# A mixture-of-experts layer whose weights arrive in transfers of 2 MB into 8 slots, instead of 1 MB into 17 slots

## The chip, the cores and the metric

The kernel runs on one core of a Trainium2 chip. The metric is the device time of one execution in microseconds (us). The time before is the median of three runs.

## The reference

One transformer layer on 512 tokens of width 1024, in float32: attention and a state-space branch side by side, an output projection, and then a feed-forward part in which every token is sent to 4 of 32 experts. Nearly all of the bytes and three quarters of the time are in that last part:

```python
def moe_ffn(h, w_router, b_router, w_gate, b_gate, w_up, b_up, w_down, b_down):
    logits = (t @ w_router + b_router).astype(jnp.float32)
    top_val, top_idx = lax.top_k(logits, TOP_K)            # TOP_K = 4 of 32
    top_w = jax.nn.softmax(top_val, axis=-1)
    ...
    def expert_block(args):
        xb, e = args                                       # rows of one expert
        g = xb @ w_gate[e] + b_gate[e]                     # 1024 x 1024
        u = xb @ w_up[e] + b_up[e]                         # 1024 x 1024
        g = jnp.minimum(g, SWIGLU_LIMIT)
        u = jnp.clip(u, -SWIGLU_LIMIT, SWIGLU_LIMIT)
        act = g * jax.nn.sigmoid(SWIGLU_ALPHA * g) * (u + 1.0)
        return act @ w_down[e] + b_down[e]                 # 1024 x 1024
```

Every expert has three matrices of 1024 x 1024 float32, 4 MB each. All 32 experts are read, so 384 MB pass from HBM to the core's memory once.

## The kernel before

The kernel is written engine by engine with explicit semaphores. Its first part (some 350 us) computes attention and the state-space branch. Then the router sorts the experts by how many tokens they got, and the expert part runs over 32 positions `j`, one expert at each. An expert's tokens are counted in groups of 32; a position has a fixed number of groups, in this order (a constant of the program, `GROUPS_AT`):

```python
[3, 3, 2, 3, 2, 3, 3, 2, 3, 3, 2, 3, 2, 3, 2, 2, 4, 2, 2, 4, 2, 2, 4, 2, 2, 2, 5, 2, 1, 5, 1, 1]
```

**TensorE.** The products of position `j` come in stages: gate of `j`, up of `j`, down of `j-1`. A stage runs through the 1024 rows of its matrix in 8 blocks of 128 (`k`), and for each block and each group it issues matmuls on the block's 1024 columns. The tokens are the stationary operand, the weights stream. A stage with 5 groups is done as two visits, 4 groups and then 1, both over the same weights. Small pieces of other work (transposes of the next tokens, one-hot products that sort them) are hooked in at fixed blocks `k`, and they stay at the same blocks.

**The weights.** A matrix is cut into pieces of `KP` blocks of 128 rows; before, `KP = 2`, so a piece is 256 rows, 1 MB, and `PIECES = 4` make a matrix. `STREAM` lists all pieces in the order of use: 384 of them before. Piece `n` goes into slot `n % NRING`, with `NRING = 17`; `RING_AT` says which part of the memory `ring` (and, for one slot, `rest`) a slot is. The text counts pieces of 1 MB from 0, before and after.

**The queue of loads.** SyncE (SP) issues all the loads of weights, in the order of `STREAM`, from one instruction stream. Before it issues a load it waits until the slot's last piece is used up (`piece_used`): for the last piece of a stage that is the end of the stage, for the others a semaphore that TensorE raises after the last visit's last matmul on that piece. A load raises a semaphore of its slot when it has landed whole, and TensorE waits for that at the piece's first block (`pe.wait_ge(s_raw[slot], ...)`, in `product`). The first loads are issued during the first part of the kernel, as the memory under their slots comes free, by the `load(n, ...)` calls that stand one by one in the code.

**The other engines.** After gate and up, VectorE and ScalarE compute the activation. After down, VectorE adds the bias, ScalarE scales the rows (L990), and GpSimd (POOL) adds them into the output with an indirect DMA for each group (L752, "scatter" below), and fetches the next tokens' rows with another (L740, "gather"). The next position's result may only be written over `yrow` when the scatters before have landed.

Of the kernel before, what the change touches and what calls it, by code (L numbers as in the profile page):

```python
# [14 lines left out]
P = 128  # L15
SEQ, DM = 512, 1024
NT = SEQ // P
KT = DM // P
# [16 lines left out]
DE = DM  # L35
# [1 line left out]
LIMIT, ALPHA = 7.0, 1.702  # L37
GRID_W = 64
IW = 52
KP = 2  # L40
PIECES = KT // KP
NRING = 17
SLOT = 4096
NQ = 4
QW = DM // NQ
# [93 lines left out]
UNITS = product_units()  # L139
STREAM = weight_stream()  # L140
SETS = 3
RING_AT = (0, 1, 16, 4, 5, 14, 15, 6, 7, 8, 9, 12, 13, 2, 3, 10, 11)
OVER_USES = [("d", 0), ("r", 0), ("x", 0), ("x", 1), ("a", 0), ("a", 1)]


# [96 lines left out]
def hybrid_layer(nc, d, out, hn):  # L242
    ctx = ExitStack()
    with ctx:
# [4 lines left out]
        big = ctx.enter_context(nc.sbuf_tensor("ring", [P, 8 * SLOT], F32))  # L249
# [55 lines left out]
        xs_w = take(NT * SW)  # L305
# [41 lines left out]
        bias_x, hT_x = xpad_w[:, 0:3 * QW], xpad_w[:, 3 * QW:4 * QW]  # L347
        btab, onehot_x = bias_w[:, 0:3 * QW], bias_w[:, 3 * QW:3 * QW + NT * TOK]
        onehot = const[:, 0:NT * P]
        slots = [big[:, n * KP * DE:(n + 1) * KP * DE] for n in range(16)] + [xs_w]  # L350
        pieces = [cut(slots[n], KP, DE) for n in RING_AT]

        rt = qT_w.rearrange("p (a b) -> p a b", b=P)
# [109 lines left out]

        WEIGHTS = ("w_gate", "w_up", "w_down")

        def piece_source(m, e, r):

            return d[WEIGHTS[m]][0, e].rearrange("(r p k) n -> r p k n", p=P, k=KP)[r]

        BIASES = ("b_gate", "b_up", "b_down")  # L470

# [118 lines left out]
        def _(sp):  # L590
            def load(n, e):

                m, j, r = STREAM[n]
                turn, slot = at_piece[m, j, r]
                if turn:
                    piece_used(sp, n - NRING)
                sp.dma_start(pieces[slot], piece_source(m, e, r)).then_inc(s_raw[slot], 16)  # L597

            sp.dma_start(const, d["const"]).then_inc(s_const, 16)
            for t in range(NT):  # L600
# [23 lines left out]
            sp.dma_start(w_out, w_out_d).then_inc(s_wout, 16)  # L624
            sp.dma_start(wr, d["w_router"][0].rearrange("(k p) n -> p k n", p=P)).then_inc(s_wr, 16)
            load(0, 0)
            load(1, 0)

            wait_full(sp, f"sb{NT - 1}")
            sp.dma_start(gffn, bc(d["norm_ffn"][0])).then_inc(s_gffn, 16)  # L630
            for t in range(NT):
                if t == NT - 1:

                    sp.wait_ge(s_ys, NT)
                    wait_full(sp, f"yf{NT - 1}")
                    for n in (2, 3, 4):
                        load(n, 0)
                    wait_full(sp, f"p{NPAIR - 1}b")
                    load(5, 0)
                    sp.wait_ge(s_of, NPAIR)  # L640
                    load(6, 0)
                wait_taken(sp, f"op{t}a")
                wait_taken(sp, f"op{t}b")
                sp.dma_start(out_d[t * P:(t + 1) * P, :], x1[:, t, :]).then_inc(s_ost, 16)
                if t == NT - 1:
                    for n in range(7, 13):
                        load(n, STREAM[n][1])
                sp.wait_ge(s_h, t + 1)
                sp.dma_start(hn_d[t * P:(t + 1) * P, :], hrw).then_inc(s_hst, 16)

            sp.wait_ge(s_ost, 16 * NT)
            for n in (13, 14):
                load(n, STREAM[n][1])
            sp.wait_ge(s_hst, 16 * NT)
            wait_full(sp, f"lg{NT - 1}")
            for n in (15, 16):
                load(n, STREAM[n][1])

            held = {}
            for n in range(NRING, len(STREAM)):  # L660
                m, j, r = STREAM[n]
# [8 lines left out]
            def over_loads(q):  # L670

                sp.wait_ge(s_done, q + 1)
                e = over_expert(sp, q)
                for m in range(3):
                    src = d[BIASES[m]][0, e]
                    for k in range(NQ):
                        sp.dma_start(bias_x[k * TOK:(k + 1) * TOK, m * QW:(m + 1) * QW],
                                     bc(src[k * QW:(k + 1) * QW], TOK)).then_inc(s_bover, 16)
                for m in range(3):
                    for r in range(PIECES):  # L680
                        turn, slot = over_piece(q, m * PIECES + r)
                        sp.dma_start(pieces[slot], piece_source(m, e, r)).then_inc(s_raw[slot], 16)

            overflow(sp, over_loads)

# [807 lines left out]
        def _(pe):  # L1493
# [246 lines left out]
                                dmask[vi.b][0:c, 0:vi.G, :].rearrange("p a b -> p (a b)"), start=True, stop=True), use)  # L1740

            def kp_rows(ap, blocks):
                return ap.rearrange("p (r i k) -> p r i k", r=blocks, k=KP)

            def turn_rows(vi):

                pe.wait_ge(s_gath[vi.b], 16 * (vi.gathers + 1))
                c = vi.G * TOK
                for h in range(2):
                    use = vi.turns["x", h]  # L1750
                    ps = turning(use)
                    for k in range(4):
                        r, kk = divmod(4 * h + k, KP)
                        last = T.transpose(ps[:, k * c:(k + 1) * c], kp_rows(hrow[vi.b][0:c, :], PIECES)[:, r, :, kk],  # L1754
                                           ident[0:c, 0:c])
                    turned(last, use)

            def turn_act(vi):

                pe.wait_ge(s_act_, vi.n + 1)  # L1760
                for h in range(last_part(vi) + 1):
                    use = vi.turns["a", h]
                    ps = turning(use)
                    rows = kp_rows(ub_b[vi.b][:, 0:vi.G * QW], vi.G)
                    for n in range(min(2, vi.G - 2 * h) * KP):
                        g, kk = divmod(n, KP)
                        last = T.transpose(ps[:, n * P:(n + 1) * P], rows[:, 2 * h + g, :, kk], ident)
                    turned(last, use)

# [116 lines left out]
```

## Time and profile before

| | us |
|---|---|
| median of 3 runs | 1445.22 (1445.13 to 1448.4) |
| the profiled execution, its own time | 1445.26 |
| its span, first to last instruction | 1443.4 |
| TensorE matmul busy | 1309.5 (91%) |
| TensorE loading its stationary operand (PEld, overlapped) | 810.8 (56%) |
| VectorE busy | 443.7 (31%) |
| ScalarE busy | 220.2 (15%) |
| GpSimd busy | 193.3 (13%) |
| DMA, mean over the span | 309 GB/s of 446.16 MB |
| TensorE clock, mean granted | 0.969 |

TensorE's busy time is the time in which at least one matmul was in flight, which is not the same as running at its peak. The DMA share of a stretch is that of the 16 DMA engines; it can come out slightly over 1. "SPq" is the instruction queue of SyncE, and a row of it is a load being issued.

### The profile page before, as it was taken

Reading aid. Unit: us, or ns where it says so; the run is one execution under the profiler, and the core shown is the slowest. Engines: PE = TensorE matmul, PEld = TensorE weight load, DVE = VectorE, ACT = ScalarE, POOL = GpSimd, SP = SyncE. Lnnn points to the kernel's source line nnn. Section 1 sums busy time; section 2 is a strip of 40 time slices with the busy share of each in tenths; the row PEclk is TensorE's granted clock in tenths of the full one; section 3 lists DMA queues with packets and bytes.
Section 4 is the critical chain, followed back from the end, with each engine's and each line's share of the span. In section 5 each row is a group of like instructions: output and inputs, shape, how many; then the busy total and the mean of one; then the engine's idle time right before and its main releaser. Section 6 shows DMA issues by size and latency. Waiting matters only on the chain.

```text
span 1443.4 us, 40133 instructions
## 1 busy us (share of the span) xinstructions
PE 1309.5 (91%) x18029; PEld 810.8 (56%) x18029; DVE 443.7 (31%) x1030; ACT 220.2 (15%) x491; POOL 193.3 (13%) x148
## 2 busy tenths in 40 slices
PE   5999989996799999999998988999989989995992
PEld 3466676664556666666555555655656655663651
DVE  3653576553322222222221211221222221311211
ACT  2123244331101111000100110110010101101100
POOL 0000310000101211111221111121121131011021
PEclk9999999998799999999999999999999999997996
DMA  8000320018899999999999999999999999999692
GB/s 347 2 1 0 153 99 1 30 42 337 311 335 380 392 387 382 391 393 399 397 394 401 398 411 396 410 400 399 411 396 405 408 395 408 403 402 384 263 408 92
DMA packets 79342, 446.16 MB, mean 309 GB/s; under 512 B 13218, under 2 KB 21474, under 8 KB 30018
## 3 DMA queue, kind: packets, MB, share of 16 engines
q1 hardware_dynamic: 64050, 426.37, 73.4%
q0 software_dynamic: 15120, 17.20, 5.6%
q8 instruction: 144, 2.36, 0.7%
q14 instruction: 28, 0.23, 0.0%
HBM read 433.29 MB, written 14.94 MB: 311 GB/s over the span
## 4 chain that ended last, share of the span: by engine, by line
PE 45%; SPq 41%; DMA 5%; issue 3%; DVE 3%; POOL 1%; ACT 1%; DVEq 0%; POOLq 0%; ACTq 0%
SPq L597 41%; PE pair L1795 22%; PE pair L1549 8%; PE pair L1533 4%; PE pair L1510 2%; DMA out<-rest 2%; DMA rest<-in_w_gate 2%; PE pair L1641 2%; DVE rest L1033 1%; PE pair L1754 1%; PE pair L1653 1%; POOL ring L700 1%; PE pair L1730 1%; PE pair L1697 1%; POOL out L752 1%
## 5 line engine op out<-in xcount | busy, mean ns | idle before, releaser
L1795 PE MATMUL pair<-ring,rest 128*32 128x256 f32 x14832 | 840.3, 381 | 34.4 <-DMA ring<-in_w_down 16.4
L1795 PEld LDWEIGHTS pair<-ring,rest 128*32 128x32 f32 x14832 | 479.4, 110 | 343.8 <-issue 25.8
L1033 DVE TENSOR_TENSOR rest<-pair,rest 128x512 f32<-128x512 f32 (+5 forms) x122 | 90.7, 743 | 491.6 <-PE pair L1795 428.4
L752 POOL DMA_INDIRECT out<-rest x82 | 128.3, 1564 | 805.5 <-ACT rest L990 739.4
L1549 PE MATMUL pair<-ring 128*128 128x512 f32 (+1 forms) x320 | 125.3, 550 | 0.0
L990 ACT ACTIVATE rest<-rest 128x256 f32<-128x256 f32 x82 | 36.5, 500 | 560.8 <-DVE rest L1033 560.8
L1549 PEld LDWEIGHTS pair<-ring 128*128 128x128 f32 x320 | 60.3, 190 | 60.4 <-issue 58.8
L1033 DVE TENSOR_TENSOR rest<-rest 128x512 f32<-128x512 f32 (+7 forms) x98 | 62.4, 650 | 34.8 <-ACT rest L972 26.7
L1795 PE MATMUL pair<-rest 128*32 128x256 f32 x912 | 55.7, 384 | 16.2 <-DVE rest L1033 13.0
L972 ACT ACTIVATE rest<-rest 128x512 f32<-128x512 f32 (+3 forms) x34 | 24.4, 718 | 292.2 <-DVE rest L1342 292.2
L1754 PE MATMUL pair<-rest 64*128 64x64 f32 (+3 forms) x272 | 41.3, 295 | 16.2 <-ACT rest L982 14.9
L1533 PE MATMUL pair<-ring 128*128 128x512 f32 x128 | 55.4, 594 | 0.0
L1754 PEld LDWEIGHTS pair<-rest 64*128 64x128 f32 (+3 forms) x272 | 35.9, 212 | 30.0 <-issue 28.6
L1510 PE MATMUL pair<-rest,ring 128*128 128x128 f32 (+1 forms) x193 | 29.2, 301 | 24.1 <-DMA ring<-in_ssm_norm 11.3
L1309 DVE TENSOR_SCALAR rest<-pair 64x1 int32<-64x1 f32 (+3 forms) x34 | 5.2, 152 | 146.3 <-issue 137.6
L1795 PEld LDWEIGHTS pair<-rest 128*32 128x32 f32 x912 | 28.7, 110 | 36.5 <-DVE rest L1033 13.4
L740 POOL DMA_INDIRECT rest<-normed_rows,rest x34 | 34.8, 1025 | 98.0 <-DVE rest L1309 67.3
L1322 DVE TENSOR_SCALAR rest<-pair,rest 128x2 int32<-128x2 f32 (+3 forms) x34 | 7.5, 221 | 130.4 <-PE pair L1739 130.4
L1510 PEld LDWEIGHTS pair<-rest,ring 128*128 128x128 f32 (+1 forms) x193 | 23.4, 154 | 38.0 <-issue 21.7
L700 POOL TENSOR_TENSOR ring<-rest 128x512 f32<-128x512 f32 x16 | 21.8, 1389 | 168.6 <-PE pair L1575 136.1
L964 ACT ACTIVATE rest<-pair 128x256 f32<-128x256 f32 (+3 forms) x68 | 28.2, 428 | 88.1 <-PE pair L1754 85.5
L1533 PEld LDWEIGHTS pair<-ring 128*128 128x128 f32 x128 | 24.2, 190 | 30.5 <-issue 30.5
(171 smaller groups left out, 827.6 us busy)
## 6 DMA issues: line engine op xcount, KB each, us to landing
ring<-in_w_up SPq DMA_DIRECT2D x121, 1024.0 KB
ring<-in_w_gate SPq DMA_DIRECT2D x120, 1024.0 KB
ring<-in_w_down SPq DMA_DIRECT2D x120, 1024.0 KB
rest<-in_w_gate SPq DMA_DIRECT2D x8, 1024.0 KB
rest<-in_w_down SPq DMA_DIRECT2D x8, 1024.0 KB
rest<-in_w_up SPq DMA_DIRECT2D x7, 1024.0 KB
ring<-in_w_in SPq DMA_DIRECT2D x1, 4160.0 KB, 15.5
ring<-in_x SPq DMA_DIRECT2D x8, 512.0 KB, 5.8
```

The source lines that it names most:

```text
L597: sp.dma_start(pieces[slot], piece_source(m, e, r)).then_inc(s_raw[slot], 16)
L700: nc.gpsimd.tensor_tensor(out=sm[k % 2], in0=times(mask, HPG), in1=over(da[:, c, di * SH + g * HPG:di * SH + (g + 1) * HPG], P), op=ALU.mu ...
L740: p.indirect_dma_start(out=hrow[vi.b][0:c, :], out_offset=None, in_=hn_d, in_offset=bass.IndirectOffsetOnAxis(ap=idx_g[vi.b][0:c, :].bitca ...
L752: p.indirect_dma_start(out=out_rows, out_offset=bass.IndirectOffsetOnAxis(ap=sidx[vi.ring][:, g:g + 1].bitcast(I32), axis=0), in_=yrow[:, ...
L990: ins = nc.scalar.activation(y, y, ACT.Copy, scale=wv[vi.ring][:, g:g + 1])
L1033: return v.tensor_tensor(out=out, in0=a, in1=b, op=op)
L1510: last = T.transpose(ps[:, n * P:n * P + k], a, ident[0:k, 0:k])
L1533: last = T.matmul(ps[:, :], w_in[:, k, XBC0 + ch * P:XBC0 + (ch + 1) * P], hTm[:, k, :], start=(k == 0), stop=(k == KT - 1))
L1549: last = T.matmul(ps[:, 0:b - a], src[:, k, t * P:(t + 1) * P], w[:, k, a:b], start=(k == 0), stop=(k == KT - 1))
L1641: last = T.matmul(bank[7][:, head * HD:(head + 1) * HD], probsT[p % 2 * 2 + h][:, kt, :], vs[:, kt, kv * HD:(kv + 1) * HD], start=(kt == 0 ...
L1754: last = T.transpose(ps[:, k * c:(k + 1) * c], kp_rows(hrow[vi.b][0:c, :], PIECES)[:, r, :, kk], ident[0:c, 0:c])
L1795: last = T.matmul(ps[q * TOK:(q + 1) * TOK, g * QW:(g + 1) * QW], x, pieces[slot][:, kk, q * QW:(q + 1) * QW], start=(k == 0 and g % 2 == ...
```

## The change

`KP` becomes 4: a piece is now 512 rows, 2 MB, and two of them make a matrix. `NRING` becomes 8, so the ring holds 16 MB, where it held 17. `RING_AT` names the eight 2 MB parts of `ring`; the 1 MB slot in `rest` is no longer used. The source of a piece is described so that each partition still receives, for every block of 256 rows, two rows that lie side by side in HBM: a transfer is 128 partitions x 2 runs of 8 KB, where it was 128 partitions x 1 run of 8 KB. Transposes of the tokens keep their arithmetic of two (`k=2` written out), so the products are the same. The first loads are issued at the same places of the program, regrouped.

```diff
-KP = 2
+KP = 4
 PIECES = KT // KP
-NRING = 17
+NRING = 8
...
-RING_AT = (0, 1, 16, 4, 5, 14, 15, 6, 7, 8, 9, 12, 13, 2, 3, 10, 11)
+RING_AT = (0, 2, 7, 3, 4, 6, 1, 5)
...
-        slots = [big[:, n * KP * DE:(n + 1) * KP * DE] for n in range(16)] + [xs_w]
+        slots = [big[:, n * KP * DE:(n + 1) * KP * DE] for n in range(NRING)]
         pieces = [cut(slots[n], KP, DE) for n in RING_AT]
...
+        def halves(piece):
+            return piece.rearrange("p (a k) n -> p a (k n)", a=2)
+
         def piece_source(m, e, r):
 
-            return d[WEIGHTS[m]][0, e].rearrange("(r p k) n -> r p k n", p=P, k=KP)[r]
+            return d[WEIGHTS[m]][0, e].rearrange("(r a p k) n -> r p a (k n)", a=2, p=P, k=KP // 2)[r]
...
-                sp.dma_start(pieces[slot], piece_source(m, e, r)).then_inc(s_raw[slot], 16)
+                sp.dma_start(halves(pieces[slot]), piece_source(m, e, r)).then_inc(s_raw[slot], 16)
...
             load(0, 0)
-            load(1, 0)
...
-                    for n in (2, 3, 4):
-                        load(n, 0)
+                    load(1, 0)
                     wait_full(sp, f"p{NPAIR - 1}b")
-                    load(5, 0)
                     sp.wait_ge(s_of, NPAIR)
-                    load(6, 0)
+                    load(2, 0)
...
-                    for n in range(7, 13):
+                    for n in range(3, 6):
                         load(n, STREAM[n][1])
...
-            for n in (13, 14):
-                load(n, STREAM[n][1])
+            load(6, STREAM[6][1])
...
-            for n in (15, 16):
-                load(n, STREAM[n][1])
+            load(7, STREAM[7][1])
```

The queue of SyncE around the start of the expert part, where the first slots are used again; `ring` and `rest` are the memories, `in_w_gate`, `in_w_up` and `in_w_down` the three weights, L597 the loads of weights. Before:

```order
L649 DMA normed_rows<-ring 128x1024
L597 DMA ring<-in_w_up 128x2048 x3
L597 DMA ring<-in_w_down 128x2048 x3
L597 DMA rest<-in_w_down 128x2048
L571 TENSOR_LOAD rest
L571 ISA x2
L597 ISA
L597 DMA ring<-in_w_gate 128x2048
```

The same place after the change, where L600 are the loads of weights:

```order
L649 DMA normed_rows<-ring 128x1024
L600 DMA ring<-in_w_up 128x2x2048 x2
L600 DMA ring<-in_w_down 128x2x2048 x2
L574 TENSOR_LOAD rest
L574 ISA x2
L600 ISA
L600 DMA ring<-in_w_gate 128x2x2048
L600 ISA
```

What was two loads is one load of two runs per partition, and the four loads of a matrix are two. No load has passed another kind of instruction. The first load that has to wait for a slot to be used up is piece 17 before (the second of the four loads of `in_w_down`, behind piece 16 which goes into the seventeenth slot), and pieces 16 and 17 together after.

## Rows read from the trace of the kernel before

**Rows 1.** TensorE's waits, 383 to 690 us, all of them: total, times, longest us

```profile
PE pair L1767 <- DVE rest L1360: 1.4, 1, 1.4
```

**Rows 2.** TensorE's waits, 690 to 1212 us: total, times, longest us

```profile
PE pair L1795 <- DMA ring<-in_w_down: 16.4, 19, 2.0
PE pair L1795 <- DMA ring<-in_w_up: 11.3, 9, 2.0
PE pair L1739 <- DMA ring<-in_w_up: 4.7, 5, 1.3
PE pair L1795 <- DMA ring<-in_w_gate: 3.8, 6, 0.6
```

**Rows 3.** TensorE's waits, 1212 to 1443 us

```profile
PE pair L1754 <- ACT rest L982: 14.9, 1, 14.9
PE pair L1795 <- DVE rest L1033: 13.0, 1, 13.0
```

**Rows 4.** Stretches: length, busy PE PEld DVE ACT POOL, PEclk, DMA share, GB/s

```profile
383.00:413.00 30.00, 28.62 (x488) 17.56 (x483) 7.24 (x19) 2.69 (x5) 1.08 (x2) 1.00 0.90 330
413.00:430.00 17.00, 17.00 (x302) 10.34 (x295) 4.32 (x11) 1.61 (x3) 0.84 (x1) 1.00 0.93 342
430.00:566.00 136.00, 136.00 (x2342) 82.71 (x2336) 34.21 (x90) 15.53 (x33) 25.45 (x18) 1.00 1.03 388
690.00:1212.00 522.00, 480.22 (x8061) 290.21 (x8064) 121.55 (x329) 53.37 (x109) 81.70 (x58) 1.00 1.02 402
```

**Rows 5.** SyncE's waits in 380-430, 430-560, 560-690 and 1200-1400 us

```profile
SPq L597 <- PE pair L1795: 54.8, 16, 16.4
...
SPq L597 <- PE pair L1795: 94.9, 50, 3.4
...
SPq L597 <- PE pair L1795: 0.5, 1, 0.5
...
SPq L597 <- PE pair L1795: 89.5, 40, 15.9
```

**Rows 6.** Timeline of SyncE: the issues of pieces 25 to 28, one by one

```profile
408.54 0.33 SPq L597 DMA_DIRECT2D ring<-in_w_up  x1
411.13 0.33 SPq L597 DMA_DIRECT2D ring<-in_w_up  x1
414.63 0.33 SPq L597 DMA_DIRECT2D ring<-in_w_up  x1
417.22 0.34 SPq L597 DMA_DIRECT2D ring<-in_w_down  x1
```

**Rows 7.** Timeline of TensorE, pieces 306 to 309: start, us, [idle before <- releaser]

```profile
1206.78 1.93 PE L1795 MATMUL pair<-ring,rest 128*32 128x256 f32 x32 [0.53 <-DMA ring<-in_w_down]
1209.27 1.93 PE L1795 MATMUL pair<-ring,rest 128*32 128x256 f32 x32 [0.56 <-DMA ring<-in_w_down]
1211.87 1.94 PE L1795 MATMUL pair<-rest 128*32 128x256 f32 x32 [0.67 <-DMA rest<-in_w_gate]
1213.74 0.74 PE L1767 MATMUL pair<-rest 128*128 128x128 f32 x4
1214.41 1.94 PE L1795 MATMUL pair<-rest 128*32 128x256 f32 x32
```

**Rows 8.** The chain that ended last, at piece 308: start, us, what

```profile
1184.00 27.74 DMA rest<-in_w_gate
```

**Rows 9.** DMA queue q1 in 1417.0 to 1417.2 us: packets, MB, share of 16 engines

```profile
q1 hardware_dynamic: 2, 0.00, 0.6%
```

**Rows 10.** Timeline of SyncE from piece 361 on, to piece 383

```profile
1343.92 2.06 SPq L597 DMA_DIRECT2D ring<-in_w_up  x3
1346.51 18.36 SPq L597 DMA_DIRECT2D ring<-in_w_down  x4
1365.62 2.87 SPq L597 DMA_DIRECT2D ring<-in_w_gate  x4
```

**Rows 11.** Timeline of TensorE where pieces 364 and 380 are first used

```profile
1376.67 7.55 PE L1795 MATMUL pair<-ring,rest 128*32 128x256 f32 x136
...
1423.37 3.66 PE L1795 MATMUL pair<-ring,rest 128*32 128x256 f32 x64 [1.06 <-issue]
```

**Rows 12.** The chain that ended last: three waits for scatters

```profile
1298.99 12.94 DMA out<-rest
...
1402.37 13.00 DMA out<-rest
...
1423.77 3.77 DMA out<-rest
```

**Rows 13.** DMA queues in 1299 to 1312 us, during the first of them

```profile
q1 hardware_dynamic: 596, 4.36, 82.8%
q0 software_dynamic: 551, 0.50, 23.9%
```

**Rows 14.** Stretches, as Rows 4: a 4 MB transfer, 1 MB transfers alone, the clock

```profile
171.00:186.00 15.00, 13.87 (x114) 13.28 (x113) 14.31 (x16) 4.78 (x8) 8.14 (x6) 1.00 1.04 407
672.00:689.00 17.00, 17.00 (x305) 10.29 (x307) 4.75 (x10) 2.06 (x5) 0.64 (x1) 1.00 1.01 416
1312.00:1321.00 9.00, 7.41 (x54) 4.68 (x58) 3.33 (x15) 3.16 (x7) 2.62 (x2) 0.51 0.95 365
```

More of the change, by code:

```diff
@@ L681, in over_loads @@
                         turn, slot = over_piece(q, m * PIECES + r)
-                        sp.dma_start(pieces[slot], piece_source(m, e, r)).then_inc(s_raw[slot], 16)
+                        sp.dma_start(halves(pieces[slot]), piece_source(m, e, r)).then_inc(s_raw[slot], 16)
             overflow(sp, over_loads)
@@ L1742, in kp_rows @@
             def kp_rows(ap, blocks):
-                return ap.rearrange("p (r i k) -> p r i k", r=blocks, k=KP)
+                return ap.rearrange("p (r i k) -> p r i k", r=blocks, k=2)
             def turn_rows(vi):
@@ L1752, in turn_rows @@
                     for k in range(4):
-                        r, kk = divmod(4 * h + k, KP)
-                        last = T.transpose(ps[:, k * c:(k + 1) * c], kp_rows(hrow[vi.b][0:c, :], PIECES)[:, r, :, kk],
+                        r, kk = divmod(4 * h + k, 2)
+                        last = T.transpose(ps[:, k * c:(k + 1) * c], kp_rows(hrow[vi.b][0:c, :], KT // 2)[:, r, :, kk],
                                            ident[0:c, 0:c])
@@ L1764, in turn_act @@
                     rows = kp_rows(ub_b[vi.b][:, 0:vi.G * QW], vi.G)
-                    for n in range(min(2, vi.G - 2 * h) * KP):
-                        g, kk = divmod(n, KP)
+                    for n in range(min(2, vi.G - 2 * h) * 2):
+                        g, kk = divmod(n, 2)
                         last = T.transpose(ps[:, n * P:(n + 1) * P], rows[:, 2 * h + g, :, kk], ident)
```

## The prediction

> **What bounds the kernel now.** I first looked for who waits for weights. TensorE's waits, cut into three stretches, give the picture. From 383 to 690 us it never waits for a transfer; its one idle stretch of note is 1.4 us [rows 1]. From 690 to 1212 us all its long waits are for landing weights; the four rows shown are 36 us and the smaller ones bring it to about 42 [rows 2]. After 1212 us it waits 14.9 and 13.0 us for ScalarE and VectorE, and not for weights [rows 3].
>
> Then I asked what the transfers do meanwhile. In 690 to 1212 us the DMA engines are busy all the time and move 402 GB/s; from 430 to 566 us they are as busy (388 GB/s), although TensorE is busy too; only before that are they short of work, at 330 and 342 GB/s and a share of 0.90 and 0.93 [rows 4]. SyncE's waits say why: until 430 us, and mostly until 560, each load waits for TensorE to use up the slot; from 560 to 690 there is one such wait of 0.5 us, and for 690 to 1200 the query had no row at all. They come back after 1200 us (89.5 us) [rows 5].
>
> So the expert part is one chain with three links. Until about 430 us TensorE frees slots and the stream of weights follows it. From there to 1212 us the stream runs by itself at its full rate, first with data in reserve, then with TensorE waiting for it. At 1211.87 us TensorE starts position 26, which has 5 groups [rows 7], and from there to the end TensorE and its scatters set the time. The load it started on had been issued at 1184.00 us and took 27.74 us to land [rows 8]: some ten pieces were queued ahead, so what SyncE does late by a few us there costs nothing. A delay of the stream before 430 us, or of the landing at 1212 us, is passed on to the end in full; elsewhere it is not.
>
> **The change part by part.**
>
> *Fewer slots and coarser release, at the start of the stream.* Before, piece n is issued when n-17 is used up. After, pieces n and n+1 (n even) go out together when both n-16 and n-15 are used up, which is the moment at which piece n+2 was issued before. So the first block of each load goes out two issues later, and the second block one issue later. Pieces 25 to 28 were issued at 408.54, 411.13, 414.63 and 417.22 us [rows 6]: an issue is 2.6 to 3.5 us. One piece transfers in 2.5 us (1209.27 to 1211.87 is 2.6, and 1211.87 to 1214.41 is 2.54) [rows 7]. Where the stream was starved, the second block of a pair ends later by one issue plus the block ahead of it, 2.6 + 2.5 = 5.1 us. Where there already was a block in reserve, it ends later by one issue alone, 2.6 us. By the shares of rows 4 the stream passes from the one to the other about 413 to 430 us. I take the middle, **+3.8 us**, and keep 0 (the reserve was already deeper) to 5.1 for the range. The seventeenth slot that is lost is in this sum: it is piece 16, no longer on board when TensorE starts.
>
> *After 430 us.* The later issues of the same rule cost nothing while loads are queued: at 1184 us the issue stands 27.74 us ahead of the landing [rows 8], and a pair goes out at most two pieces, some 6 us, later. If that cover were gone, each us late would be a us of the total, up to 1212.
>
> *Waiting for the whole 2 MB at 1212 us.* Position 26 can now start only when 308 and 309 have landed. TensorE touched 309 at 1214.41, 2.54 us after 308 [rows 7]; it had not waited for it, so the landing lay at or before that. Before the landing of 308, pieces came each 2.5 us, so 309 is expected at 1214.4: **+2.5 us** (bounds 0 and 2.6). What follows needs a pair each 7 us of work (four groups: two pieces of 3.5), and a pair lands in 5, so it happens once.
>
> *Half the completion writes.* Each load ends on each DMA engine with a small write to its semaphore. Two such packets alone in 0.2 us are 0.6% of 16 engines' time [rows 9]: 0.006 x 16 x 200 / 2 = 9.6 ns. From piece 26 to 308 there are 141 fewer on each engine: **-1.4 us**.
>
> *Work on TensorE, VectorE and the rest.* The matmuls, the hooks and their blocks are the same; 192 waits and as many signals fewer are not on a path with a row: in 383 to 690 us, where data was always there, no idle stood before a piece [rows 1]. 0.
>
> *The end.* After 1212 us slots are late by the same rule, most of all behind stages of 5 groups, whose four pieces are released together. The worst is the pair 364, 365: before, 364 was issued at 1346.51 us and the next three only around 1363; all four ended by 1364.9 [rows 10]. After, the pair waits for the issue time of 366, about 1363.7. Two blocks are 5 us, plus a start of about 1, plus the completion: landed by 1371. TensorE comes to piece 364 inside the row that starts at 1376.67 us [rows 11], about 2 us into it, so 7 to 8 us are left. From there the stream carries one block more than before (364 was already on board), so the last pair lands some 3 us later than the last piece did; it was on board by about 1417.5 (two completion packets at 1417.0 to 1417.2 are its last [rows 9]), and the last stage runs its four pieces in 3.66 us from 1423.37 [rows 11]: the last pair is wanted at 1425.2, 4.7 us after 1420.5. So the end is covered, by 5 us at the tightest, and moves as a block. 0; if the cover fails, 1 us for 1 us.
>
> *Sum.* 3.8 + 2.5 - 1.4 = +4.9 us. The profiled execution took 1445.26 us, of which 1443.4 is its span; the median of the runs is 1445.22, so nothing is to be corrected. **1450.2 us.**
>
> **A rule weighed against the rows.** A 4 MB transfer (of the output weights, in runs 512 KB apart) moved 407 GB/s, and 1 MB pieces by themselves 416 GB/s [rows 14]; so neither a larger transfer nor one that jumps between blocks is seen to run at another rate, and the sum has 0 for it. The Trainium skill (DMA: Bandwidth & Descriptors, section Bandwidth) gives 341 GB/s for single transfers of 1 MB and 425 GB/s for 16 MB, from a fixed 2 us each. By that rule doubling the size would cut the stream's time noticeably; the rows disagree, since 1 MB pieces queued behind each other lose nothing of that kind.
>
> **The rivals.**
>
> *A: the stream gets faster.* Per-load losses that I can't see are halved. For: the mean of 402 GB/s in 690 to 1212 us is under the 416 of the clean stretch [rows 4, 14]. Against: the scatters and gathers explain that, and rows 14 show no gain by size. Were it 2% (402 to 410), the 800 us from 413 to 1212 would shrink by 16 us, well inside the 42 us that TensorE waits: 1450.2 - 16 = 1434. It is faster than before by over 0.3% as soon as the rate gains 1.2%. Chance 0.10.
>
> *B: scatters land later.* The waits for scatters are on the chain, 12.94 and 13.00 us for four each while weights flow, against 3.77 for one alone [rows 12]. In the first, the scatters' queue q0 has 23.9 parts to 82.8 of the weights' q1 [rows 13]. So of 3.2 us per scatter 0.8 is its own and 2.4 is turns given to the weights. If a turn doubles with the transfer, a scatter takes 5.6 us, four take 22.5, and both waits grow by 9.5: 1450.2 + 19 = 1469. Against: the runs of 8 KB stay as they are; a turn may well be one run. Chance 0.12. The Trainium skill (DMA: Bandwidth & Descriptors, section Queues, rings and completion order) has the engines change queues only after a whole packet of typically 9 to 17 descriptors, and by that rule a load of twice the descriptors would take longer turns; no row here shows whose packets they are.
>
> *C: the clock falls.* Two short pauses per 2 MB become one: 2.0 us at most before [rows 2], so up to 3 or 4 us after. The clock stayed at 1.00 (2.4 GHz) throughout 690 to 1212 us [rows 4], but stood at 0.51, near its 1.2 GHz level, for the 7.2 us of work after the 13 us wait [rows 14]. Were it low when position 26 begins, that costs half of 7.2, 3.6 us: 1454. Elsewhere the stream hides it. Chance 0.10.
>
> *D: the reserve hides the start.* If the stream was saturated before 413 us, the 3.8 falls away: 1445.3 + 2.5 - 1.4 = 1446.4, no change that can be told. For: TensorE's own pace there is close to the stream's. Against: the share of 0.93 up to 430 us. Chance 0.25.
>
> **How the numbers follow.** The forecast case, 1449.0 to 1451.5 by its bounds (one issue, or one issue and a block, with the 2.5 and the -1.4), has 0.43. About 0.3% (4.3 us) is what a measurement can tell from no change, so the line is at 1449.6. The forecast case gives 0.33 to slower and 0.10 to same; D 0.25 to same; B and C 0.22 to slower; A 0.10 to faster. Together 0.10, 0.35, 0.55. The range of 1440 to 1464 takes in the forecast case, C, D and the milder parts of A and B.
>
> **What would show it.** (1) TensorE's waits for weights: none before about 670 us, then pauses about twice as long and half as many, some 45 us in all. (2) Position 26 begins at 1216 to 1217 us. (3) The rest, from there to the end, is as long as before, 1443.4 - 1211.9 = 231.5 us of span; a longer one means B, seen in waits of over 20 us for `out<-rest`, or a failed cover at the end, seen as waits for weights after 1217. (4) GB/s in the middle stretch 402 within 1%; 406 or more is A. (5) A granted clock under 1.00 between 690 and 1212 us is C. The prediction is wrong if the rate of the stream moves with the transfer's form, each 1% being 8 us.

## The result: slower by 0.6 to 0.7%, and where it went

The changed kernel took 1454.35 us (median of 8 runs) beside 1445.18 us for the kernel before: ratio 1.0069, 95% interval [1.0051, 1.0087]. Measured again on another occasion: 1452.33 us beside 1445.31, ratio 1.0059 [1.0043, 1.0074]. The ratios are those on record with their intervals; the quotients of the medians are 1.0063 and 1.0049. Its first profiled execution took 1454.72 us, with a span of 1452.8 us; the second 1451.29 us, span 1449.5.

The stretches of the changed kernel, with the columns of [rows 4], come first:

```profile
383.00:413.00 30.00, 28.62 (x488) 17.50 (x480) 7.24 (x19) 2.68 (x5) 0.97 (x1) 1.00 0.78 290
413.00:430.00 17.00, 17.00 (x301) 10.35 (x294) 3.59 (x10) 1.61 (x3) 0.96 (x1) 1.00 1.00 362
690.00:1212.00 522.00, 488.54 (x8109) 294.28 (x8105) 122.37 (x329) 55.38 (x114) 83.24 (x59) 0.98 1.02 402
```

Until 413 us the stream of weights moves 290 GB/s, where it moved 330; the DMA share has gone from 0.90 to 0.78. In the middle the rate is 402 GB/s, as before. So the bytes are late from the start and not slower on the way. The timeline of SyncE shows the new steps of the start. Each load is now 2 MB, so the row with `x2` is two loads and 4 MB, and the time from 404.42 to 411.96 and on to 424.46 is what TensorE needs to use up whole pairs. Before, pieces went out singly, 2.6 to 3.5 us apart [rows 6].

```profile
404.42 0.38 SPq L600 DMA_DIRECT2D ring<-in_w_gate  x1
411.96 6.46 SPq L600 DMA_DIRECT2D ring<-in_w_up  x2
424.46 0.38 SPq L600 DMA_DIRECT2D ring<-in_w_down  x1
```

SyncE's waits in 380-430, 560-690, 690-1200 and 1200-1400 us, which answer to [rows 5]:

```profile
SPq L600 <- PE pair L1793: 54.0, 7, 19.4
...
SPq L600 <- PE pair L1793: 27.9, 9, 6.0
...
SPq L600 <- PE pair L1793: 97.1, 38, 6.9
...
SPq L600 <- PE pair L1793: 145.0, 29, 20.9
```

After 560 us SyncE now waits for slots again and again (97.1 us in 38 waits between 690 and 1200 us), where before it hardly did. It looks bad and costs nothing there: DMA share and GB/s are those of before, because a load still has 33 us from issue to landing. A wait of an engine that runs far ahead is no loss.

TensorE's waits, first 383 to 690 us [rows 1], then 690 to 1212 us [rows 2], then 1220 to 1453 us [rows 3]:

```profile
PE pair L1793 <- DMA ring<-in_w_gate: 3.0, 1, 3.0
PE pair L1793 <- DMA ring<-in_w_down: 2.8, 3, 1.9
PE pair L1765 <- DVE rest L1358: 1.4, 1, 1.4
...
PE pair L1793 <- DMA ring<-in_w_down: 17.8, 9, 3.2
PE pair L1793 <- DMA ring<-in_w_up: 10.2, 6, 2.6
PE pair L1793 <- DMA ring<-in_w_gate: 3.9, 4, 1.4
...
PE pair L1752 <- ACT rest L980: 15.8, 1, 15.8
PE pair L1793 <- ACT rest L980: 13.8, 1, 13.8
PE pair L1793 <- issue: 1.1, 1, 1.1
```

There are fewer and longer waits for weights (9 for `w_down`, where there were 19), and none near the end. TensorE's timeline at the start of the expert part and around position 26 [rows 7]:

```profile
379.13 6.06 PE L1793 MATMUL pair<-ring,rest 128*32 128x256 f32 x76 [0.63 <-issue]
...
1208.96 3.66 PE L1793 MATMUL pair<-ring,rest 128*32 128x256 f32 x64 [0.46 <-DMA ring<-in_w_down]
1213.76 3.66 PE L1793 MATMUL pair<-ring,rest 128*32 128x256 f32 x64 [1.14 <-DMA ring<-in_w_down]
1218.82 1.93 PE L1793 MATMUL pair<-ring,rest 128*32 128x256 f32 x32 [1.40 <-DMA ring<-in_w_gate]
```

and the same first row in the kernel before:

```profile
378.08 6.27 PE L1795 MATMUL pair<-ring,rest 128*32 128x256 f32 x76 [0.63 <-issue]
```

Position 26 begins at 1218.82 us, 6.95 us later than before (1211.87). 1.05 us of that existed already when the expert part began (379.13 against 378.08). That start varies by itself: in thirteen profiles of kernels that share everything ahead of it except the first loads it lay between 375.5 and 379.1 us. So I compare **the time from the first matmul of the expert part to the start of position 26**: 833.8 us before, 839.7 after, so 5.9 us; 839.1 in the second profile, so 5.3.

The rest, from position 26 to the end of the span, took 234.0 us (before 231.5). The chain that ended last has here, with [rows 8] and [rows 12]:

```profile
1185.63 33.06 DMA ring<-in_w_gate
...
1305.93 13.80 DMA out<-rest
...
1409.99 13.87 DMA out<-rest
...
1425.23 6.35 PE pair L1793 x64
...
1433.44 3.75 DMA out<-rest
```

The two long waits for scatters are 0.9 us longer each. So 9.4 us of difference between the two profiled spans are 1.05 ahead of the expert part, 5.9 up to position 26, 1.7 in scatter waits, and 0.7 in the work between them. The 64 matmuls behind the second wait alone took 6.35 us instead of 5.17; in the second profile they took 5.17 again.

### The profile page after: what moved, and what is told of

It reads as the page before. It is cut to its first block, busy times and chain, and to the rows that moved or that the text cites. A ratio compares the mean times of both kernels' runs of the same rounds, so it can differ in the third digit from the quotient of the medians.

```text
span 1452.8 us, 39702 instructions
## 1 busy us (share of the span) xinstructions
PE 1316.4 (91%) x18029; PEld 813.2 (56%) x18029; DVE 443.8 (31%) x1030; ACT 220.0 (15%) x491; POOL 193.1 (13%) x148
## 4 chain that ended last, share of the span: by engine, by line
PE 64%; DMA 21%; SPq 8%; DVE 3%; issue 2%; POOL 1%; ACT 1%; DVEq 0%; POOLq 0%; ACTq 0%
PE pair L1793 39%; DMA ring<-in_w_gate 10%; PE pair L1547 8%; SPq L600 7%; DMA ring<-in_w_up 5%; PE pair L1531 4%; DMA ring<-in_w_down 3%; DMA out<-rest 2%; PE pair L1508 2%; PE pair L1752 2%; PE pair L1639 2%; PE pair L1765 1%; PE pair L1728 1%; DMA ring<-in_w_in 1%; DVE rest L1031 1%
## 5 line engine op out<-in xcount | busy, mean ns | idle before, releaser
L1793 PE MATMUL pair<-ring,rest 128*32 128x256 f32 x15744 | 897.2, 385 | 56.2 <-DMA ring<-in_w_down 21.8
L1793 PEld LDWEIGHTS pair<-ring,rest 128*32 128x32 f32 x15744 | 510.1, 111 | 389.9 <-issue 45.2
L1531 PEld LDWEIGHTS pair<-ring 128*128 128x128 f32 x128 | 24.2, 190 | 30.5 <-issue 30.5
L1367 DVE STREAM_SHUFFLE rest<-rest 128x256 f32<-128x256 f32 (+1 forms) x64 | 37.9, 592 | 0.0
L1297 DVE TENSOR_SCALAR rest<-rest 128x64 f32<-128x64 f32 (+3 forms) x136 | 26.3, 259 | 25.0 <-DVE rest L1031 19.0
```

The costliest lines, as they stand in the source:

```text
L1367: lk(v.stream_shuffle(out=bias_x[:, a * QW:b * QW], in_=btab[:, a * QW:b * QW], mask=[j] * TOK))
L1531: last = T.matmul(ps[:, :], w_in[:, k, XBC0 + ch * P:XBC0 + (ch + 1) * P], hTm[:, k, :], start=(k == 0), stop=(k == KT - 1))
L1793: last = T.matmul(ps[q * TOK:(q + 1) * TOK, g * QW:(g + 1) * QW], x, pieces[slot][:, kk, q * QW:(q + 1) * QW], start=(k == 0 and g % 2 == ...
```

## The experiments

All kernels were timed beside the kernel before on the same chip. Its median there was 1445.18 us for ring16, pair_issue, pair_wait and ring7, 1445.31 for after_again, split26, one_two_one and half_loads, 1446.80 for rows_by_two and rows_by_four, and 1447.48 for the last two; each ratio is to its own. The columns behind the ratio are read from the one profiled execution: from the first expert matmul to position 26, the sum of the two long scatter waits in the chain (before: 12.94 + 13.00), and from position 26 to the end of the span.

| kernel | us | ratio, 95% interval | to position 26 | against before | scatters | from position 26 to the end |
|---|---|---|---|---|---|---|
| before | 1445.18 | | 833.8 | | 25.9 | 231.5 |
| changed | 1454.35 | 1.0069 [1.0051, 1.0087] | 839.7 | +5.9 | 27.7 | 234.0 |
| after_again | 1452.33 | 1.0059 [1.0043, 1.0074] | 839.1 | +5.3 | 26.9 | 232.8 |
| ring16 | 1447.83 | 1.0016 [0.9996, 1.0036] | 836.5 | +2.7 | 25.9 | 232.6 |
| pair_issue | 1452.72 | 1.0043 [1.0022, 1.0065] | 838.4 | +4.6 | 26.0 | 231.1 |
| pair_wait | 1447.85 | 1.0011 [0.9993, 1.0028] | 836.3 | +2.5 | 27.2 | 234.3 |
| ring7 | 1462.23 | 1.0121 [1.0074, 1.0168] | 844.8 | +11.0 | 27.4 | 237.2 |
| split26 | 1451.42 | 1.0056 [1.0034, 1.0077] | 837.9 | +4.1 | 27.1 | 232.5 |
| one_two_one | 1444.63 | 0.9992 [0.9977, 1.0007] | 832.7 | -1.1 | 26.0 | 232.4 |
| half_loads | 1951.50 | 1.3456 [1.3398, 1.3513] | | | | |
| rows_by_two | 1443.70 | 0.9972 [0.9945, 0.9999] | 833.8 | 0.0 | 24.6 | 230.9 |
| rows_by_two_again | 1442.71 | 0.9975 [0.9957, 0.9993] | 833.4 | -0.4 | 24.2 | 230.3 |
| rows_by_four | 1457.91 | 1.0063 [1.0040, 1.0086] | 849.4 | +15.6 | 20.5 | 231.0 |
| two_in_four | 1450.94 | 1.0037 [1.0017, 1.0057] | 839.9 | +6.1 | 24.0 | 231.3 |

Two profiles of one kernel differ by 0.4 to 0.6 us to position 26, by up to 0.7 in the scatter waits and by up to 1.2 in the last column. The medians are worse: single executions of the kernel before lay between 1442 and 1454 us.

### One slot less (ring16)

```diff
-NRING = 17
+NRING = 16
...
-RING_AT = (0, 1, 16, 4, 5, 14, ...
+RING_AT = (0, 1, 4, 5, 14, ...
...
```

> One part alone: 16 slots of 1 MB, everything else as before. Theory 1 (the loss is made where the stream of weights is starved, until about 430 us, and the start of position 26 passes it on): each piece goes out one issue of TensorE later, 2.6 us, so position 26 begins at 1214.5 instead of 1211.9 and the time is 1447.8 us. Clock 1.00 in 690 to 1212 us and scatter waits of 12.9 and 13.0 us as before. Theory 2 (what was lost is the seventeenth slot, the form of the loads matters little): most of the 7 us of the changed kernel, 1451 us or more. Theory 3 (the form of the loads costs it all: 2 MB transfers and their completion): no change, 1445.2 us.

Position 26 came 2.7 us later (2.6 expected), the median rose by 2.6 us; the interval of its ratio still takes in 1, so it is the profile that shows it, where the spread is 0.6. The seventeenth slot is worth one issue of TensorE, since it decides how far the stream is ahead when it stops being starved.

### Issue in pairs (pair_issue)

```diff
-                if turn:
+                if turn and n % 2 == 0:
                     piece_used(sp, n - NRING)
+                    piece_used(sp, n + 1 - NRING)
...
```

The 16 slots of ring16 are in this kernel too.

> 16 slots of 1 MB, and the two loads of a pair are both issued only when both slots are used up; transfers stay 1 MB with a semaphore each, and TensorE waits for each by itself. Theory 1: the lag of the whole start, 5.1 us and up to 1 us more; nothing for the whole pair at position 26, and the lag does not shrink in the middle, since there are as many completion writes as before: position 26 begins at 1217 to 1218 us and the time is 1450.4 to 1451.4 us, 2.6 to 3.6 us over the kernel with 16 slots. No pause of TensorE over 2.3 us in 690 to 1212 us, clock 1.00. Theory 3 (form of the loads): as the kernel with 16 slots, within 1 us.

4.6 us in the profile, where 5.1 to 6.1 was expected, and a median of 1452.72 us for 1450.4 to 1451.4. Its timeline at position 26, against [rows 7], has the old rhythm of single waits near 0.6 us; only the time has moved:

```profile
1212.39 1.93 PE L1796 MATMUL pair<-ring,rest 128*32 128x256 f32 x32 [0.56 <-DMA ring<-in_w_down]
1214.97 1.93 PE L1796 MATMUL pair<-ring,rest 128*32 128x256 f32 x32 [0.65 <-DMA ring<-in_w_gate]
```

So the lost slot and the rule of issue together, in transfers of 1 MB, make four fifths of the delay up to position 26; over ring16 the rule adds 1.9 us, somewhat less than one issue. Its median (1452.72) is higher than its profiled execution (1447.94) for reasons the profile can't show; I go by the profile's 4.6.

### Wait for pairs (pair_wait)

```diff
-                    if first:
-                        pe.wait_ge(s_raw[slot], 16 * (pturn + 1))
+                    if first and r % 2 == 0:
+                        for pturn, sl in (piece(m, r), piece(m, r + 1)):
+                            pe.wait_ge(s_raw[sl], 16 * (pturn + 1))
```

> The kernel before, with 17 slots and loads of 1 MB, but TensorE waits for both pieces of a pair before it begins the first. Theory 1: position 26 begins 2.5 us later, at 1214.4 us, and the time is 1447.7 us. In the middle the pauses are as in the changed kernel, up to 3.0 to 3.3 us, and the clock falls there some times to its half (mean 0.98), which costs nothing that shows at position 26. Theory 4 (the fallen clock costs time, the stream does not hide it): 1449 us or more, position 26 at 1216 or later.

2.5 us to position 26, as expected. The median of 1447.85 us, near the expected 1447.7, is no second proof: in the profile 2.8 us more come behind position 26, and the expert part happened to begin 2.5 us earlier than in the kernel before (375.54 against 378.08). The rows at position 26 show two things:

```profile
1205.31 3.66 PE L1796 MATMUL pair<-ring,rest 128*32 128x256 f32 x64 [1.18 <-DMA ring<-in_w_down]
1211.82 2.57 PE L1796 MATMUL pair<-rest 128*32 128x256 f32 x32 [2.85 <-DMA ring<-in_w_gate]
1214.33 1.13 PE L1767 MATMUL pair<-rest 128*128 128x128 f32 x4
```

The wait is 2.85 us, where before it was 0.67. And the 32 matmuls behind it take 2.57 us instead of 1.94, the four transposes 1.13 instead of 0.74: the granted clock was at half from 1212.8 to 1216.3 us, just behind the pause, exactly where it is not hidden (rival C's place). These two rows cost 1.0 us of the 234.3 us from position 26 to the end, and the next 32 matmuls (2.40 us instead of 1.94) another half. In the middle, where the stream has slack, the clock fell twice and nothing is seen of it at position 26.

### One pair fewer (ring7)

```diff
-NRING = 8
+NRING = 7
...
-RING_AT = (0, 2, 7, 3, 4, 6, 1, 5)
+RING_AT = (0, 2, 7, 3, 4, 6, 1)
...
```

> The changed kernel with 7 slots of 2 MB instead of 8. Theory 1: a pair goes out two issues of TensorE later still, 5.2 us where the stream is starved, which now lasts longer than to 430 us; position 26 begins at about 1224 us and the time is about 1459.6 us. The cover of the last stages (5 to 6 us) gets short there; a wait for weights after 1224 us would add to it. Theory 5 (the start had a reserve that swallowed most of it, and the 7 us have another source): under 1457 us.

844.8 us to position 26, 5.1 to 5.8 us more than the changed kernel in its two profiles (5.2 expected): two issues again. The time is 2.6 us over the expected 1459.6, and TensorE's waits after 1222 us name what is new, a wait for weights and a longer gap at the end:

```profile
PE pair L1792 <- issue: 3.3, 1, 3.3
PE pair L1792 <- DMA ring<-in_w_up: 1.8, 1, 1.8
```

So the cover of the last stages, put at 5 us at its tightest with 8 slots, is used up with 7, as far as the one wait of 1.8 us for weights shows; what makes the gap of 3.3 us (1.1 before), no row says.

### Position 26 begins on the first half (split26)

```diff
+                if n == SPLIT:
+                    for h, s in enumerate((s_raw[slot], s_half)):
+                        sp.dma_start(halves(pieces[slot])[:, h:h + 1],
+                                     piece_source(m, e, r)[:, h:h + 1]).then_inc(s, 16)
+                    return
...
+                        if first and kk == KP // 2 and vi.j == 26 and m == 0 and r == 0:
+                            pe.wait_ge(s_half, 16)
```

> The changed kernel, but the first load of position 26 (the pair 308, 309) goes as two transfers of 1 MB with a semaphore each, and TensorE begins on the first. Theory 1: position 26 begins 2.5 us earlier than in the changed kernel, and the time is 1451.9 us. Counted from the first matmul of the expert part, which lay between 375.5 and 379.1 us in the profiles so far, it begins 837.2 us later (839.7 in the changed kernel, 833.8 before). If the wait for the whole pair costs nothing because TensorE catches up later, the time stays at 1454.4 us.

Only 1.2 to 1.8 us came back, not 2.5. The timeline says why:

```profile
1206.00 3.66 PE L1801 MATMUL pair<-ring,rest 128*32 128x256 f32 x64 [0.56 <-DMA ring<-in_w_down]
1210.66 5.39 PE L1801 MATMUL pair<-ring,rest 128*32 128x256 f32 x96 [1.00 <-DMA ring<-in_w_down]
```

The x96 are the 64 matmuls of the pair before and the first 32 of position 26, with no wait between: the first half had landed. (Position 26 has no row of its own here; its start, 1214.1 us, is 32 matmuls before the end of this one.) TensorE was held by its wait for the whole pair before it. With pairs throughout, the last wait costs 1.5 us, and 1 us of the 2.5 belongs to the one ahead.

### 1 MB where it counts, 2 MB between (one_two_one)

```diff
+RING_16 = tuple(s for s in RING_AT if s < 16)
+SWITCH = 4 * NRING
+DOUBLE = range(80, 300, 2)
+def slot_of(n):
+    return RING_AT[n % NRING] if n < SWITCH else RING_16[(n - SWITCH) % 16]
...
```

> 1 MB pieces in 17 slots while the stream is starved, as before; from piece 68 the same pieces in 16 slots, from 80 to 299 in transfers of 2 MB that are issued and waited for whole, and 1 MB again from piece 300, so also at position 26. Theory 1: neither the start nor position 26 loses anything and 110 completion writes go: 1.06 us less, position 26 begins 832.7 us after the first matmul of the expert part and the time is 1444.1 us. The clock dips of the changed kernel appear in the middle without a price. If transfers of 2 MB cost something by themselves in the full stream, it is over 1446 us.

No loss: ratio 0.9992, so a transfer of 2 MB costs nothing in the full stream; the whole price is at the start and at the place where TensorE catches up for the last time. Its 832.7 us is what was expected with 110 fewer completion writes. That is 1.1 us under 833.8, not much over the 0.6 between two profiles of one kernel; the next runs test the price of a write directly and find none, so what made the 1.1 us stays open.

### The price of a completion write (half_loads, rows_by_two, rows_by_four)

half_loads, and under it rows_by_two (rows_by_four has 4 for 2, and 64 for 32):

```diff
-                sp.dma_start(pieces[slot], piece_source(m, e, r)).then_inc(s_raw[slot], 16)
+                for a in (0, 64):
+                    sp.dma_start(pieces[slot][a:a + 64],
+                                 piece_source(m, e, r)[a:a + 64]).then_inc(s_raw[slot], 16)
...
+                for a in range(2):
+                    sp.dma_start(pieces[slot][a::2], piece_source(m, e, r)[a::2]).then_inc(s_raw[slot], 16)
...
-                        pe.wait_ge(s_raw[slot], 16 * (pturn + 1))
+                        pe.wait_ge(s_raw[slot], 32 * (pturn + 1))
```

> The kernel before, with each piece of 1 MB loaded as two transfers of 64 rows, so there are twice as many completion writes; packets, slots and waits stay. If a completion write costs the stream 9.6 ns (which is behind the 1.4 us that the changed kernel was to gain), the stream loses 9.6 ns for each of some 280 pieces between 430 us and the start of position 26: that start lies 2.7 us later from the first matmul of the expert part (836.5 instead of 833.8), and the time is 1447.9 us. If the write costs nothing in a full stream: 833.8 and 1445.2 us. If the size of a load sets the stream's rate by a fixed cost of each (rival A): 1450 us or more.

It answered another question. All its stretches are starved though the DMA share is full:

```profile
690.00:1212.00 522.00, 367.97 (x5524) 199.53 (x5528) 81.53 (x212) 37.05 (x75) 54.89 (x39) 0.94 1.02 273
```

273 GB/s instead of 402, by writing to rows 0 to 63 in one transfer and 64 to 127 in the next. The Trainium skill (SBUF — State Buffer, section Door 1: The DMA port swizzle) has a DMA's bandwidth depend on how many of 16 ports its partitions reach, and by its formula 64 neighbouring rows reach 8. The trace agrees in direction. That the rate is more than half of 402 may come from neighbouring transfers, to the two halves, being under way together; no run shows that.

> The kernel before, with each piece of 1 MB loaded as two transfers, one of the even and one of the odd rows, so each transfer writes across the whole memory and not into one half of its rows. Twice as many completion writes, packets of 8 KB as before. If the half rows made the transfers slow (8 KB packets of 0.50 us instead of 0.32 with 64 neighbouring rows), that is gone. If a completion write costs 9.6 ns of the full stream: position 26 begins 836.5 us after the first matmul of the expert part and the time is 1447.9 us. If it costs nothing: 833.8 and 1445.2 us. If each transfer has a fixed cost of its own in the stream, 1450 us or more.

Every second row restores the rate (401 GB/s in 690 to 1212 us). And with twice as many completion writes position 26 begins 833.8 us after the first matmul, to the tenth as before; 833.4 in the second profile below. The two rows:

```profile
377.65 6.54 PE L1798 MATMUL pair<-ring,rest 128*32 128x256 f32 x72 [0.63 <-issue]
...
1211.45 1.94 PE L1798 MATMUL pair<-rest 128*32 128x256 f32 x32 [0.64 <-DMA rest<-in_w_gate]
```

836.5 was expected at 9.6 ns each. **So a completion write costs the full stream nothing that can be seen.** The row on which I had priced it [rows 9] gives its duration on an engine that has nothing else to do, and that isn't its price in a full queue. That packets overlap there would explain it; no run shows how.

> The same with four transfers for each piece, of every fourth row, so four times as many completion writes as before. At 9.6 ns each: 8.2 us more of stream from 430 us to position 26, which begins 842.0 us after the first matmul of the expert part; the time is 1453.4 us. If they cost nothing: 833.8 and 1445.2 us. With a fixed cost of each transfer well over 10 ns: more than 1456 us.

15.6 us later, well over 8.2, but this is another bound. The rows of SyncE's timeline in the starved start are groups of four issues that nothing blocks, and then 16 in a row:

```profile
383.83 2.38 SPq L598 DMA_DIRECT2D ring<-in_w_down  x4
...
391.33 10.78 SPq L598 DMA_DIRECT2D ring<-in_w_gate  x16
```

0.6 to 0.7 us per issue, 2.4 to 2.7 us for 1 MB, where the stream needs 2.5. The rate falls to 386 GB/s in the middle. The chain at position 26 points the same way: the load that it waits for landed 5 us after its issue, where before it took 27.74 [rows 8], so hardly anything was queued ahead of it.

```profile
1220.46 5.09 DMA rest<-in_w_gate
```

SyncE's issue as the cause fits in size and in this row, but no run tested it, and it leaves open why the DMA share stays at 1.02 in the middle while the rate is lower. The kernel therefore says nothing about the price of a completion write. Single 1 MB issues at the start take 0.33 us [rows 6].

### Transfer size and the scatters (two_in_four, rows_by_two_again, after_again)

two_in_four is the changed kernel with each 2 MB sent as four transfers; slots, issue in pairs and waits stay.

```diff
-                sp.dma_start(halves(pieces[slot]), piece_source(m, e, r)).then_inc(s_raw[slot], 16)
+                for h in range(2):
+                    for a in range(2):
+                        sp.dma_start(halves(pieces[slot])[a::2, h:h + 1],
+                                     piece_source(m, e, r)[a::2, h:h + 1]).then_inc(s_raw[slot], 16)
```

> The changed kernel with its 8 slots, its issue in pairs and its waits for 2 MB, but each 2 MB goes as four transfers of 0.5 MB (even and odd rows of each block). Only the size of a transfer differs. If the size of a transfer lengthens the scatters' turns a little (rival B in small), the two long waits near the end, which added up to 28.9 to 29.6 us in the three profiles with 2 MB transfers and to 26.6 us with 0.5 MB, come down to about 26.6 us, and the time is some 2.5 us under the changed kernel's on the same chip. Theory 1 alone (size of the transfers without effect): waits of 29 us in sum and no difference. Position 26 begins 839.1 to 839.7 us after the first matmul of the expert part in both cases.

To position 26 nothing changes (839.9). The scatter waits in its chain fall from 13.80 and 13.87 us to these:

```profile
1303.99 11.69 DMA out<-rest
1406.99 12.26 DMA out<-rest
```

In the table's terms: 26.9 to 27.7 us in the four profiles with 2 MB, 25.9 or 26.0 in four of the five with 1 MB, 24.0 to 24.6 in the three profiles with 0.5 MB. The fifth with 1 MB is pair_wait at 27.2, which I can't explain. two_in_four is the clean pair: same kernel, only the size differs, 3 to 3.7 us less. (The expectations count TensorE's two idle rows instead, as [rows 3]: 14.9 + 13.0 = 27.9 us before, 29.6 and 28.9 changed, 25.9 in two_in_four, 26.6 and 26.1 in rows_by_two.)

Not all of it reaches the end. From position 26 on two_in_four takes 231.3 us, 1.5 to 2.7 less than the changed kernel; its chain has one more scatter wait, which the other chains haven't:

```profile
1421.02 5.68 DMA out<-rest
```

In the medians the gain isn't clear of noise: its interval [1.0017, 1.0057] overlaps with both of the changed kernel's.

> The changed kernel once more, for a second profile beside the first. Theory 1: position 26 begins 839.7 us after the first matmul of the expert part (5.9 us more than in the kernel before), whatever that matmul's own start is, and if the first profile's late start of 379.1 us was chance, 1.0 us of its difference to the kernel before goes. Scatter waits: if the 0.9 us by which each of the two was longer belongs to the change, 13.8 and 13.9 us again; if not, between 12.9 and 13.9.

5.3 us instead of 5.9 to position 26, 26.9 us of scatter waits: between the two expectations.

> The kernel before with each 1 MB piece as two transfers (even and odd rows), once more, with more rounds. If shorter transfers shorten the scatters' waits: ratio 0.997 to 0.999 to the kernel before, sum of the two long waits near the end 26 to 27 us (27.9 before), position 26 at 833.8 us after the first matmul of the expert part. If the first ratio of 0.997 was chance: 1.000.

0.9975 [0.9957, 0.9993], after 0.9972 [0.9945, 0.9999]: **the only version that beats both kernels**, by about 0.25%. In its profile the scatter waits are 1.8 us shorter, of which 1.2 are left from position 26 to the end (230.3 us for 231.5); to position 26 it gains 0.4, which is within the spread. The medians gain 3.1 and 4.8 us, more than the profiles show.

## Why the prediction came near, point by point

It said 1450.2 us and slower by 0.34%; measured were 0.6 to 0.7%. The mechanism held: lost at the start, passed through the full stream, and handed on at position 26. The sum up to there, +4.9 for +5.9 and +5.3, is nearer than its terms, and that part is luck: the first term was low, the second was counted in full where only a part of it adds, and the third took off 1.4 us that don't exist. By its own steps:

- **Fewer slots and coarser release, +3.8.** Right in kind, low in size. One slot is one issue (2.6 expected, 2.7 in ring16); the pair rule and the slot together are 4.6 (pair_issue), and two issues more are 5.1 to 5.8 (ring7, 5.2 expected). The upper bound, "one issue plus the block ahead of it", was nearly true and I had averaged it with a case that hardly occurred, because I took the share of 0.93 in 413 to 430 us as a half-full stream. This term was mis-sized.
- **Waiting for the whole 2 MB, +2.5.** 2.5 in pair_wait. In the changed kernel itself, undoing it at position 26 gave back 1.2 to 1.8 (split26).
- **Half the completion writes, -1.4.** Wrong. Doubling them cost 0.0 and -0.4 us, where 2.7 was due, and the changed kernel with four times its own number (two_in_four) reached position 26 at the same time. This step failed: a duration of an idle engine was taken as a price in a full queue.
- **What was to show it.** The waits for weights came to about 41 us (45 expected; before, the rows named for weights add up to 40, not quite the 42 of the prediction), in fewer and longer pauses; the rate held; position 26 began at 1218.8 and 1216.7 us (1216 to 1217 expected). Two things were not as written: waits for weights began at some point before 690 us already, 5.8 us of them, and the end was longer. The three terms together: +4.9 predicted, +5.9 and +5.3 measured. 4.6 and 2.5 would add up to 7.1, so 1 to 2 us of one are within the other: split26 shows 1 us of it.
- **The middle, 0.** Right: one_two_one, and 402 GB/s in both.
- **The end, 0.** The cover held with 8 slots; with 7 it was gone. But the end was not as long as before: 234.0 and 232.8 us instead of 231.5. Longer scatter waits are 1.7 and 1.0 us of that, rival B in small. With the start of the expert part this is why the total lies 2 to 4 us over the forecast.
- **Rival A (faster by size).** Refuted: 402 GB/s for 2 MB and 1 MB, 401 for 0.5 MB.
- **Rival B (scatters' turns double).** It was to cost 19 us; it cost 1.0 to 1.7. The direction is real (two_in_four), the doubling isn't: from 0.5 to 2 MB, a factor of four, the waits grow by a seventh. By the Trainium skill's rule (DMA: Bandwidth & Descriptors, section Queues, rings and completion order) an engine changes queues only after a whole packet; turns of the whole transfer are not what the runs show.
- **Rival C (the clock falls).** It happened six times in the middle of the changed kernel, at about 713.8, 775.3, 840.1, 983.4, 1082.4 and 1181.4 us, each time in or just behind a pause of 2.3 to 3.2 us, and the stream hid it, as it was to "elsewhere". A window that holds one, with the columns of [rows 4] (granted clock 0.62):

```profile
1082.50:1087.00 4.50, 3.87 (x48) 1.98 (x52) 0.00 (x0) 0.00 (x0) 0.00 (x0) 0.62 1.01 403
```

and TensorE's timeline in it:

```profile
1083.13 4.99 PE L1793 MATMUL pair<-ring,rest 128*32 128x256 f32 x64 [3.19 <-DMA ring<-in_w_down]
```

64 matmuls take 4.99 us instead of 3.66. At position 26 the pause was 1.40 us and the clock stayed; in pair_wait the pause was 2.85 us and it didn't. The length of a pause doesn't settle it by itself: the changed kernel's pause of 2.38 us before 879.16 us left the clock at 1.00, and so did one of 3.40 us before 1074.63 us in pair_wait.
- **Rival D (reserve hides the start).** Refuted by ring16 and pair_issue: 2.7 and 4.6 us in their profiles.

What stays open: the first median is 9.2 us over that of before, the second 7.0. The profiles account for 6.6 (5.3 + 1.3, second profile) to 8.4 us (5.9 + 2.5) of it. The rest may lie in the start of the expert part, which differed by up to 3.6 us between executions of kernels that hardly differ ahead of it; the profiles can't show it for the other executions.

## What to carry to other kernels

A ring of buffers has its price where the stream is starved and where the consumer catches up with it for the last time: there, count one issue for every slot and somewhat less for every piece that a release is coarser (2.7 and 1.9 us here), and between the two places count nothing. Take both bounds of such a term seriously: a starved stream is starved wholly. Size of the slot, unit of release, unit of the wait and size of a transfer are four choices; a transfer of 0.5 MB cost the full stream nothing here when its rows were spread over all partitions, and the other queue's scatters landed sooner; at 0.25 MB the stream lost rate, probably because the issuing engine no longer kept up.

## What the runs showed of the hardware that I had not expected

- Transfers of 64 neighbouring rows ran at 273 GB/s, of 64 alternating rows at 401 GB/s, with packets of 8 KB in both.
- Twice as many completion writes cost the full queue nothing: 833.8 and 833.4 us to position 26 for 833.8, though one such write alone takes some 9.6 ns.
- Shorter transfers of one queue let another queue's scatters land earlier: 24.0 us against 26.9 to 27.7 for the two waits, at 0.5 MB instead of 2 MB.
- TensorE's granted clock fell to half (1.2 GHz) at pauses of 2.3 to 3.2 us in the changed kernel; before, pauses of up to 2.0 us never brought it down between 383 and 1212 us. That is no safe limit: in ring16 one pause of 1.97 us, after others of 1 to 1.2 us, did, and in rows_by_two one of 1.46 us. Nor does a longer one always bring it down: in pair_wait TensorE ran 64 matmuls in 3.66 us, full speed, behind a pause of 3.40 us.
- An issue by SyncE took 0.33 us for 128 neighbouring rows and, when issues followed each other directly, 0.6 to 0.7 us for 32 rows, every fourth.
